# First block's attention by tile, and stick-breaking attention in twelve batches of 512 columns, in an eight-stage transformer kernel

## The chip, the cores and the metric
The kernel runs on one core of a Trainium2 chip, all in fp32. A core has TensorE (PE, matmuls), VectorE (DVE), ScalarE (ACT, activation functions), GpSimd (POOL, which here issues the gathers) and SyncE (SP, which issues the loads), 16 DMA engines, an SBUF of 128 partitions and a PSUM of eight banks of 512 fp32 columns. The engines run their own instruction streams and wait for one another on semaphores. The metric is the device time in microseconds, lower is better.

## The reference
Two transformer blocks over 256 tokens of width 1024, one batch. The change lies in the first block, which has two layers:

```python
def first_block(x, ...):
    for layer in range(2):
        if layer < 1:
            mix = _diff_attention(x, ...)          # 8 heads with two maps each, softmax, sublayer norm
        else:
            k_sb, v_sb = _shared_kv(x, w_kv_b)
            mix = _stick_breaking(x, ...)          # 16 heads of 64
        x = _layer_norm(DEEPNORM_ALPHA * x + mix, ...)
        x = _layer_norm(DEEPNORM_ALPHA * x + _peer(x, ...), ...)

# stick-breaking, for a block of 128 queries
    mask = key_pos[None, :] < t[:, None]
    z = einsum('bhqd,bhkd->bhqk', q, k_sb) * scale
    log_one_minus = where(mask, log_sigmoid(-z), 0.0)
    tail = cumsum(log_one_minus, reverse=True) - log_one_minus
    a = where(mask, exp(log_sigmoid(z) + tail), 0.0)
    out = einsum('bhqk,bhkd->bhqd', a, v_sb)
```

`_diff_attention` takes per head the difference of two softmax maps (keys of later 64-token chunks are masked), multiplies by v, divides each head's 128 outputs by their root mean square (the sublayer norm) and projects. `_peer` scores 8 heads of 2 x 128 sub-keys per token, picks 16 experts of each head by two top-16 selections, fetches a row of 2048 numbers (u and v) for each of the 128 picks, takes gelu(x.u) times a gate, and adds up the v's. The second block has four layers (selected, window, latent and again selected attention), each with an MLP of width 4096.

## The kernel before
**Layout.** T = 256 tokens are two tiles (NT = 2) of P = 128. `x` holds the tokens by partition, `xT` the same turned, `y` is 3 x 1024 columns per tile for projections. `weights` has four slots of 2 MB; a slot takes a chunk of 512 columns of a weight matrix. `arena` (8192 columns) holds attention outputs `o` or four gathered rows, `heads_arena` holds `qT` and `kT`, `scratch` small work.

**Semaphores and order.** Each engine's order is written out by hand. A planner at the top gives every PSUM use a `Group` (bank, number of its filling, number of its freeing) and every weight chunk the event after which its slot is free (`slot_release`). PE waits `bank_free(g)` before it fills and `copied(g)` where it needs the evicted data; the others wait `filled(g)`. SP issues the weight loads in program order (`load_weights`, L780).

**Building blocks.** `turns` (L870) transposes four 128x128 blocks through a bank, ACT evicts them (L1233). `project` (L883) makes one block of 512 output columns for one tile: 8 matmuls over the 1024 inputs, 16 in the trace, as each fp32 matmul shows as two. ACT evicts it to `y` (L1239) or DVE adds it to x (`add_to_x`, L1688). `project_turned` (L893) makes PEER queries already turned. `layer_norm` (L1695 to L1701) is DVE with a square root on ACT (`root`, L1243). A change of function on ACT costs a table load.

**First stage.** qkv projection of both tiles; rotation; turns; `attend(diff)` runs 32 units (16 maps x 2 tiles) as a software pipeline: scores of unit i (L916), transposes of probabilities of unit i-2 (L931), values of unit i-4 (L942), with DVE negating, masking and taking the maximum (L1654), copying (L1667) and dividing each four units (L1677, L1679), ACT exponentiating (L1251). Then DVE does the sublayer norm of tile 0 and 1 (L2068 to L2075), PE turns both, projects tile 0 and 1 (4 blocks), and `peer` begins.

**PEER stage.** Per tile: turn x, project queries, scores against the sub-keys (L1000), evictions (L1301). Then DVE routes (`route`, L1711 to L1752), POOL gathers (L2173; ten slots of 1 MB, four in `arena`, six in weight slots 1 to 3), DVE takes the products (L1770), ACT gelu (L1311) and diagonal matrices of the weights (L1320), PE mixes the v's (L1018). `PE_PICKS` says which picks PE mixes: all 16 of each head. `peer_sum` in `xT` starts as ALPHA times x (L1807); at a tile's end `add_mixed` (L1793) adds the banks to it, and a layer norm follows. Weight slots 1 to 3 are released by that norm.

**Stick attention.** PE waits for both tiles of x, turns them, projects keys and values (8 blocks) and queries (4 blocks), turns queries and keys, then `stick_attend` runs 16 heads of 384 columns (keys 0 to 127 x 256 queries, keys 128 to 255 x 128 queries):

```python
    z^T = k q^T                                   # PE, L954, L955, 64 rows deep
    l = log(1 + exp(-|z|))                        # ACT, L1266, L1268, L1278
    w = max(z, 0) + l; sp = w * mask; w = z - w   # DVE, L1842, L1843, L1845
    t = later^T sp (+ ones^T sp of later tile)    # PE, L965 to L968
    w = w - t                                     # DVE, L1851
    a = exp(w) * mask                             # ACT L1285, POOL L2196
    o += a^T v                                    # PE, L979 to L981
```

The heads' exponentials and logarithms go in fours, since each change of function reloads a table. Then turns of `o`, output projection (4 blocks), two norms, and the second PEER stage.

## Time and profile before
| | us |
|---|---|
| median of 3 runs | 3105.93 (3105.5 to 3109.35) |
| the profiled execution, its own time | 3107.64 |
| its span, first to last instruction | 3106.0 |
| PE / PEld / DVE / ACT / POOL busy | 2616.1 / 1611.5 / 1741.4 / 917.0 / 648.9 |
| mean DMA rate over the span | 247 GB/s |
| granted TensorE clock, mean | 0.953 |

The span begins with the first instruction. PE is the matmul unit, PEld its weight loads, which overlap it. A share of busy time is a mean over stages of different kinds: two PEER stages with gathers, four MLPs, and attention. The page's second part cuts the span into 40 slices of 78 us. A timeline row reads: start, duration, engine, line, operation, output<-inputs, shapes, count, and in brackets the idle time before it with what ended it.

### The profile page before, as it was taken

How to read it: one execution, taken by the hardware profiler on the slowest of the kernel's cores; microseconds unless marked ns; L12 is line 12 of the kernel's file. 1: busy time of each engine (PE TensorE's matmuls, PEld its weight loads, DVE VectorE, ACT ScalarE, POOL GpSimd, SP SyncE). 2: the span in 40 equal slices, each digit the busy share in tenths (PEclk: the TensorE clock that was granted, in tenths of full speed). 3: DMA queues.
4: the chain of work that ended last, by engine and by line, in shares of the span. 5: the costliest groups of instructions: out<-in, count | busy, mean ns of one | idle time of the engine just before them, and what ended most of it. 6: DMA issues, size and time to landing. Idle time of an engine off the chain costs nothing.

```text
span 3106.0 us, 30124 instructions
## 1 busy us (share of the span) xinstructions
PE 2616.1 (84%) x10349; PEld 1611.5 (52%) x10349; DVE 1741.4 (56%) x3866; ACT 917.0 (30%) x1914; POOL 648.9 (21%) x635
## 2 busy tenths in 40 slices
PE   7986777777779796777777788999999989998999
PEld 3553222223334662222222234798479857985698
DVE  2446777777630446777777645654455455545554
ACT  1312222222112421222222123443344354433443
POOL 0004444444410203444444411000100000001000
PEclk9998999999989698999999999999999989999999
DMA  7219999999964019999999953354335423543253
GB/s 249 82 30 399 422 421 416 389 421 421 421 268 157 1 62 414 421 421 421 386 421 421 421 204 109 121 185 154 109 124 188 151 82 122 189 159 109 96 189 108
DMA packets 209663, 767.63 MB, mean 247 GB/s; under 512 B 16435, under 2 KB 87686, under 8 KB 143750
## 3 DMA queue, kind: packets, MB, share of 16 engines
q0 software_dynamic: 73760, 536.93, 41.7%
q1 hardware_dynamic: 135782, 229.22, 22.0%
q8 instruction: 60, 0.98, 0.1%
q14 instruction: 61, 0.50, 0.0%
HBM read 765.03 MB, written 1.07 MB: 247 GB/s over the span
## 4 chain that ended last, share of the span: by engine, by line
PE 39%; DMA 6%; DVE 4%; ACT 1%; issue 1%; POOL 0%; DVEq 0%; ACTq 0%
PE psum L1056 12%; PE psum L1070 11%; PE psum L883 9%; DMA weights<-in_peer_uv,scratch 4%; DMA arena<-in_peer_uv,scratch 2%; PE psum L1018 2%; PE psum L942 1%; PE psum L870 1%; PE psum L931 1%; PE psum L920 1%; DVE heads_arena L1770 1%; PE psum L916 0%; PE psum L1034 0%; DVE arena L1679 0%; ACT scratch L1320 0%
## 5 line engine op out<-in xcount | busy, mean ns | idle before, releaser
L1018 PE MATMUL psum<-weights,scratch 128*128 128x512 f32 x1224 | 585.5, 624 | 203.6 <-ACT scratch L1320 203.6
L883 PE MATMUL psum<-weights,xT 128*128 128x512 f32 (+2 forms) x1192 | 517.8, 593 | 16.4 <-ACT xT L1233 11.4
L1018 PEld LDWEIGHTS psum<-weights,scratch 128*128 128x128 f32 x1224 | 229.4, 196 | 558.4 <-ACT scratch L1320 306.9
L1018 PE MATMUL psum<-arena,scratch 128*128 128x512 f32 x824 | 391.0, 620 | 133.6 <-ACT scratch L1320 132.9
L2173 POOL DMA_INDIRECT weights<-in_peer_uv,scratch x306 | 342.2, 1118 | 498.9 <-PE psum L1018 407.5
L1995 DVE TENSOR_TENSOR piece<-weights,piece 128x2048 fp32r<-128x2048 f32 x128 | 292.8, 2293 | 221.1 <-ACT piece L1361 221.1
L1056 PE MATMUL psum<-split_x,piece 128*128 128x256 f32 x3072 | 385.4, 286 | 6.2 <-DVE split_x L2002 6.2
L1056 PEld LDWEIGHTS psum<-split_x,piece 128*128 128x128 f32 x3072 | 383.4, 195 | 11.6 <-issue 7.6
L883 PEld LDWEIGHTS psum<-weights,xT 128*128 128x128 f32 x1192 | 228.7, 196 | 284.1 <-issue 273.5
L1070 PE MATMUL psum<-piece,hidden 128*128 128x512 f32 x1536 | 358.8, 390 | 0.0
L1311 ACT ACTIVATE scratch<-scratch 128x2 f32<-128x2 f32 x256 | 52.1, 203 | 1000.2 <-DVE heads_arena L1770 1000.2
L1018 PEld LDWEIGHTS psum<-arena,scratch 128*128 128x128 f32 x824 | 153.2, 195 | 370.0 <-ACT scratch L1320 201.6
L2173 POOL DMA_INDIRECT arena<-in_peer_uv,scratch x206 | 230.9, 1121 | 413.1 <-PE psum L1018 285.3
L1070 PEld LDWEIGHTS psum<-piece,hidden 128*128 128x128 f32 x1536 | 284.8, 188 | 56.8
L1361 ACT ACTIVATE piece<-weights 128x2048 fp32r<-128x2048 f32 x128 | 243.2, 1906 | 170.1 <-PE psum L1056 170.1
L1770 DVE SCALAR_TENSOR_TENSOR heads_arena<-weights,x 128x1024 f32<-128x1024 f32 x153 | 187.3, 1224 | 131.0 <-DMA weights<-in_peer_uv,scratch 131.0
L1770 DVE SCALAR_TENSOR_TENSOR scratch<-weights,x 128x1024 f32<-128x1024 f32 x153 | 187.4, 1225 | 89.4 <-issue 81.5
L1770 DVE SCALAR_TENSOR_TENSOR heads_arena<-arena,x 128x1024 f32<-128x1024 f32 x103 | 126.1, 1224 | 84.5 <-DMA arena<-in_peer_uv,scratch 84.4
L1320 ACT ACTIVATE scratch<-const,scratch 128x128 f32<-128x128 f32 x512 | 173.3, 386 | 0.0
L2209 POOL MEMSET heads_arena<- 64x256 f32 (+1 forms) x6 | 3.1, 521 | 776.5 <-DVE arena L1875 776.3
L1770 DVE SCALAR_TENSOR_TENSOR scratch<-arena,x 128x1024 f32<-128x1024 f32 x103 | 126.1, 1225 | 59.6 <-issue 51.2
L1239 ACT ACTIVATE y<-psum 128x512 f32<-128x512 f32 (+1 forms) x52 | 29.9, 576 | 249.3 <-PE psum L883 249.3
(206 smaller groups left out, 2346.8 us busy)
## 6 DMA issues: line engine op xcount, KB each, us to landing
weights<-in_w_up SPq DMA_DIRECT2D x64, 1024.0 KB, 5.5
weights<-in_w_down SPq DMA_DIRECT2D x64, 1024.0 KB, 4.9
weights<-in_w_qkv_a SPq DMA_DIRECT2D x6, 2048.0 KB, 20.2
weights<-in_a_w_in SPq DMA_DIRECT2D x6, 2048.0 KB, 10.4
weights<-in_peer_w_q SPq DMA_DIRECT2D x4, 2048.0 KB, 8.4
weights<-in_w_kv_b SPq DMA_DIRECT2D x4, 2048.0 KB, 12.9
weights<-in_a_w_out SPq DMA_DIRECT2D x4, 2048.0 KB, 8.6
weights<-in_b_w_in SPq DMA_DIRECT2D x3, 2048.0 KB, 10.3
```

The costliest lines, as they stand in the source:

```text
L870: mm = pe.transpose(psum[g.bank][0:rows, j * P:j * P + n], src, identity[0:n, 0:n])
L883: mm = pe.matmul(psum[g.bank][:, 0:w], xT[:, block0 + k, t * P:(t + 1) * P], c.view[:, k, c0:c0 + w], start=(k == 0), stop=(k == c.rows - 1))
L920: pe.matmul(psum[g.bank][:, 0:2 * nk], qT[:, h // 2, t * P:(t + 1) * P], paired_keys(kind, h, nk), start=True, stop=True).then_inc(psum_fi ...
L1018: mm = pe.matmul(psum[g.bank][:, :], diagonal[:, j % DIAGONALS, :], row[:, D + half * BANK:D + (half + 1) * BANK], start=(j == pe_picks(t ...
L1056: mm = pe.matmul(psum[g.bank][:, b * T:(b + 1) * T], w[a][:, k, b * P:(b + 1) * P], split_x[c][:, k, :], start=(k == 0 and (a, c) == PARTS ...
L1070: mm = pe.matmul(psum[g.bank][:, :], h[a][:, k, t * P:(t + 1) * P], w[c][:, k, half * BANK:(half + 1) * BANK], start=(first and k == 0 and ...
L1311: act.activation(gelu[:, k:k + 2], dots[:, k:k + 2], ACT.Gelu).then_inc(gelu_given.sem, 1)
L1320: act.activation(diagonal[:, j % DIAGONALS, :], identity, ACT.Copy, scale=weight[:, k:k + 1])\
L1361: act.activation(split_piece[n][0][:, :], raw_piece[n], ACT.Copy).then_inc(high_ready.sem, 1)
L1770: dve.scalar_tensor_tensor(unused[at % 2], gathered[at % GATHER_SLOTS][:, 0:D], 1.0, x[:, n // SEL, :], ALU.mult, ALU.mult, accum_out=dots ...
L1995: dve.tensor_tensor(split_piece[n][1][:, :], raw_piece[n], split_piece[n][0][:, :], ALU.subtract)\
L2173: pool.indirect_dma_start(gathered[at % GATHER_SLOTS], None, rows, bass.IndirectOffsetOnAxis(ap=expert[:, t, k:k + 1], axis=0), element_of ...
```

## The change
1. **Diff attention by tile.** `attend` on PE and DVE is called once per tile. Tile 0's sublayer norm is a generator whose six pieces DVE does inside tile 1's units (`SUBLN_STEPS`), in `y` instead of `heads_arena`; ACT takes its root after eight of tile 1's exponentials. Turns and output projection go by tile, with the turn of x tile 0 for PEER between the last two blocks.
2. **PEER entry.** `queries` and `scores_of` replace the first half of `peer`: the turn of x tile 1 comes before the scores of tile 0. The branch for picks not mixed by PE leaves, with `peer_sum`; `add_mixed` does x = ALPHA * x + bank. Weight slots 1 to 3 are released by the last mixing.
3. **Stick attention.** Twelve batches of 512 columns: for tile 0 four heads of one key tile, for tile 1 two heads of two key tiles. Keys and queries are projected turned for both tiles at once (`project_both`), ACT writes them to `kT` and to `stick_q`, where each pair of heads has its other half zeroed by POOL, so scores are 128 rows deep. The mask is a matmul of -1e30 with an identity, in fp32r, into the same bank. Values go to PSUM turned (`stick_oT`), so no turn precedes the output projection. The second halves of values, keys and queries and tile 0's output projection stand between rounds of three batches.
4. **Constants** are 256 columns narrower.

The diff, cut to its core:

```diff
+STICK_BATCHES = ((0, 0), (0, 4), (1, 0), (1, 2), (1, 4), (1, 6), (0, 8), (0, 12), (1, 8), (1, 10), (1, 12), (1, 14))
+SUBLN_STEPS, SUBLN_ROOT = (2, 4, 6, 9, 11, 13), 8
...
-                slot_release[1] = slot_release[2] = slot_release[3] = (x_ready.sem, ln_x[2 * layer + 1] + NT)
+                slot_release[1] = slot_release[2] = slot_release[3] = (value_mixed.sem, self.mixed0 + NT * SEL)
...
+                self.s = [group(2 + b % 3) for b in range(n)]
+                self.t = [group(5) for _ in range(n)]
...
+            def project_both(c, g, half):
+                bank_free(g)
+                for j in range(2):
+                    at = (2 * half + j) * P
+                    for k in range(KB):
+                        mm = pe.matmul(psum[g.bank][:, j * T:(j + 1) * T], c.view[:, k, at:at + P], xT[:, k, :],
+                                       start=(k == 0), stop=(k == KB - 1))
...
+            def stick_scores(s, b):
+                t, h = STICK_BATCHES[b]
...
+                if t == 0:
+                    pe.matmul(psum[g.bank][:, :], stick_identity[:, :], stick_masks[:, :], start=True, stop=False)
+                for j in range(2):
+                    pair, keys = (h // 2 + j, 0) if t == 0 else (h // 2, j)
...
+                    mm = pe.matmul(psum[g.bank][:, j * T:(j + 1) * T], kT[:, pair, keys * P:(keys + 1) * P], stick_q[t][:, pair, :, :],
...
+            def stick_later(s, b):
...
+                if t == 0:
+                    mm = pe.matmul(psum[g.bank][:, :], later, w, start=True, stop=True)
+                else:
+                    pe.matmul(psum[g.bank][:, T:2 * T], later, w[:, T:2 * T], start=True, stop=True)
+                    pe.matmul(psum[g.bank][:, 0:T], later, w[:, 0:T], start=True, stop=False)
+                    mm = pe.matmul(psum[g.bank][:, 0:T], ones, w[:, T:2 * T], start=False, stop=True)
...
-            attend(diff, "diff")
-            pe.wait_ge(in_ready.sem, diff_out_in + 1)
-            turns(diff_out_turn)
-            copied(diff_out_turn.last)
-            project(diff_out.blocks)
-            peer(peer0, ln_x[0])
+            attend(diff, "diff", 0, HEADS)
+            attend(diff, "diff", HEADS, NT * HEADS)
+            for t in range(NT):
+                pe.wait_ge(in_ready.sem, diff_out_in + t + 1)
+                turns(diff_out.turn[t])
+                project(diff_out.blocks[t][0:1], turned=diff_out.turn[t].done)
+                if t == NT - 1:
+                    turn_x(peer0, 0, ln_x[0])
+                project(diff_out.blocks[t][1:2])
+            queries(peer0, ln_x[0])
...
+            exps(diff, None, 0, HEADS + SUBLN_ROOT)
+            root(diff_root, PEER_HEADS)
+            exps(diff, None, HEADS + SUBLN_ROOT, NT * HEADS)
+            root(diff_root + 1, PEER_HEADS)
+            for t in range(NT):
+                turns(diff_out.turn[t])
...
+                for first in range(0, len(STICK_BATCHES), 3):
+                    batches = range(first, first + 3)
+                    softs(batches)
+                    logits(batches)
+                    less_later(batches)
```

PE's order in the stick attention is now: x turn 0, values 0 (tile 0), x turn 1, values 0 (tile 1), keys 0, queries 0, scores of batches 0 to 2, values 1 (2 blocks), later sums 0 to 2, half of keys 1, scores 3 to 5, values of 0 to 2, half of keys 1 and of queries 1, later sums 3 to 5, rest of queries 1, scores 6 to 8, values 3 to 5, later sums 6 to 8, scores 9 to 11, values 6 to 8, output block, later sums 9 to 11, output block, values 9 to 11; then the two output blocks of tile 1 with the turn of x tile 0 between. ACT's order has the same rounds: logs, Ln, evictions, Exp.

**PE, from the end of the diff attention to the first mixing.** L870/L904 are turns (by what they read: `arena` the attention's output, `x`, `heads_arena` the sub-keys), L883/L917 the output projection, L893/L927 queries, L1000/L1110 scores. Before:

```order
L942 MATMUL psum<-y,scratch 128x128 x6
L870 MATMUL psum<-const,arena 128x128 x16
L883 MATMUL psum<-weights,xT 128x512 x32
L870 MATMUL psum<-const,x 128x128 x8
L870 MATMUL psum<-const,heads_arena 128x128 x8
L893 MATMUL psum<-xT,weights 128x128 x64
L1000 MATMUL psum<-heads_arena 128x128 x16
L870 MATMUL psum<-const,x 128x128 x8
L893 MATMUL psum<-xT,weights 128x128 x64
```

And now:

```order
L976 MATMUL psum<-y,scratch 128x128 x6
L904 MATMUL psum<-const,arena 128x128 x8
L917 MATMUL psum<-weights,xT 128x512 x16
L904 MATMUL psum<-const,arena 128x128 x8
L917 MATMUL psum<-weights,xT 128x512 x8
L904 MATMUL psum<-const,x 128x128 x8
L917 MATMUL psum<-weights,xT 128x512 x8
L904 MATMUL psum<-const,heads_arena 128x128 x8
L927 MATMUL psum<-xT,weights 128x128 x64
L904 MATMUL psum<-const,x 128x128 x8
L1110 MATMUL psum<-heads_arena 128x128 x16
L927 MATMUL psum<-xT,weights 128x128 x64
```

The turns stand by tile, and both turns of x moved ahead by one step.

**PE, where the third round of stick batches begins.** L1002 and L1006 are masks, L1007 scores, L1037 values, L1019 to L1023 sums over later keys, L986 turned projections, L917 plain ones. Before, the same place had single heads in a pipeline, nine instructions to a head:

```order
L954 MATMUL psum<-heads_arena 128x256
L955 MATMUL psum<-heads_arena 128x128
L965 MATMUL psum<-arena,const 128x128
L966 MATMUL psum<-arena,const 128x128
L967 MATMUL psum<-arena,const 128x128
L968 MATMUL psum<-arena,const 128x128
L979 MATMUL psum<-y,arena 128x64
L980 MATMUL psum<-y,arena 128x64
L981 MATMUL psum<-y,arena 128x64
```

And now:

```order
L986 MATMUL psum<-xT,weights 128x256 x16
L1002 MATMUL psum<-stick_masks,stick_identity 128x512
L1007 MATMUL psum<-y,heads_arena 128x256 x2
L1002 MATMUL psum<-stick_masks,stick_identity 128x512
L1007 MATMUL psum<-y,heads_arena 128x256 x3
L1006 MATMUL psum<-stick_masks,stick_identity 128x256
L1007 MATMUL psum<-y,heads_arena 128x256
L1037 MATMUL psum<-arena,y 64x128 x12
L1019 MATMUL psum<-arena,const 128x512 x2
L1021 MATMUL psum<-arena,const 128x256
L1022 MATMUL psum<-arena,const 128x256
L1023 MATMUL psum<-arena,const 128x256
```

Between scores (L1007) and later sums (L1019) of this round stand only the value matmuls of the round before.

**DVE, inside tile 1's units of the diff attention.** L1654/L1823 is the masked maximum, L1667/L1836 the copy of transposed probabilities. Before, two units:

```order
L1654 ISA scratch,neg_max<-psum,const 128x256
L1654 ISA neg_max 128x1
L1667 COPY scratch<-psum 128x256
L1654 ISA scratch,neg_max<-psum,const 128x256
L1654 ISA neg_max 128x1
L1667 COPY scratch<-psum 128x256
```

And now:

```order
L2219 SCALAR_TENSOR_TENSOR y<-arena,lam 128x1024
L1823 ISA scratch,neg_max<-psum,const 128x256
L1823 ISA neg_max 128x1
L1836 COPY scratch<-psum 128x256
L1823 ISA scratch,neg_max<-psum,const 128x256
L1823 ISA neg_max 128x1
L1836 COPY scratch<-psum 128x256
L2221 TENSOR_TENSOR y<-y 128x1024
```

A piece of tile 0's norm over 1024 columns stands before every second or third unit.

## Rows read from the trace of the kernel before

**Rows 1.** Page, part 2: granted clock of TensorE and share of the DMA engines
```profile
PEclk9998999999989698999999999999999989999999
...
DMA  7219999999964019999999953354335423543253
```

**Rows 2.** Windows: busy PE, PEld, DVE, ACT, POOL, clock, DMA share, GB/s
```profile
262.00:551.00 289.00, 219.61 (x468) 86.04 (x466) 208.88 (x550) 65.01 (x199) 134.30 (x118) 0.98 1.00 415
...
260.00:264.00 4.00, 4.00 (x7) 1.61 (x6) 3.93 (x11) 1.30 (x6) 1.63 (x1) 0.66 0.40 152
...
923.00:996.00 73.00, 72.31 (x171) 31.90 (x170) 0.00 (x0) 6.57 (x11) 0.00 (x0) 1.00 0.45 161
1019.00:1024.00 5.00, 0.00 (x0) 0.00 (x0) 1.97 (x4) 4.49 (x9) 1.95 (x2) 0.65 0.00 0
1024.00:1085.00 61.00, 51.04 (x221) 46.01 (x222) 25.54 (x48) 23.65 (x41) 15.20 (x14) 0.55 0.00 1
```

**Rows 3.** Timeline, DVE: two units of the attention's second tile
```profile
137.56 0.42 DVE L1654 CUSTOM_DVE_ANT_0 scratch<-psum,const 128x256 f32<-128x256 f32 x1 [0.65 <-PE psum L916]
...
137.93 0.42 DVE L1667 COPY scratch<-psum 128x256 f32<-128x256 f32 x1
...
139.00 0.42 DVE L1654 CUSTOM_DVE_ANT_0 scratch<-psum,const 128x256 f32<-128x256 f32 x1 [0.65 <-PE psum L916]
```

**Rows 4.** Timeline, DVE: sublayer norm, first tile's sum and norm
```profile
153.55 1.28 DVE L2068 SCALAR_TENSOR_TENSOR heads_arena<-arena,lam 128x1024 f32<-128x1024 f32 x1
...
157.38 0.17 DVE L2071 TENSOR_SCALAR root_in<-sums 128x8 f32<-128x8 f32 x1
...
185.82 0.69 DVE L1688 SCALAR_TENSOR_TENSOR x<-x,psum 128x512 f32<-128x512 f32 x1 [6.25 <-PE psum L883]
...
190.97 1.23 DVE L1701 TENSOR_TENSOR x<-x,ln_gb 128x1024 f32<-128x1024 f32 x1
```

**Rows 5.** Timeline, PE: turns, output projection, first queries
```profile
167.64 3.39 PE L870 MATMUL psum<-const,arena 128*128 128x128 f32 x16 [15.06 <-DVE arena L2075]
171.71 27.73 PE L883 MATMUL psum<-weights,xT 128*128 128x512 f32 x64 [0.69 <-ACT xT L1233]
...
201.56 14.46 PE L893 MATMUL psum<-xT,weights 128*128 128x128 f32 x128
```

**Rows 6.** Timeline, POOL: first and eleventh gather; first of the second PEER stage
```profile
230.02 1.00 POOL L2173 DMA_INDIRECT arena<-in_peer_uv,scratch  x1 [119.82 <-DVE scratch L1752]
...
261.49 1.63 POOL L2173 DMA_INDIRECT arena<-in_peer_uv,scratch  x1 [16.98 <-PE psum L1018]
...
1151.72 0.97 POOL L2173 DMA_INDIRECT weights<-in_peer_uv,scratch  x1 [67.13 <-DVE scratch L1752]
```

**Rows 7.** Timeline, PE: last mixing, turns, twelve projection blocks, scores after a stall
```profile
894.79 3.60 PE L1018 MATMUL psum<-weights,scratch 128*128 128x512 f32 x8
905.57 3.68 PE L870 MATMUL psum<-const,x 128*128 128x128 f32 x16 [7.18 <-DVE x L1701]
909.93 85.02 PE L883 MATMUL psum<-weights,xT 128*128 128x512 f32 x192 [0.69 <-ACT xT L1233]
...
1024.17 1.22 PE L954 MATMUL psum<-heads_arena 64*128 64x256 f32 x2 [5.43 <-DVE scratch L1845]
```

**Rows 8.** Timeline, PE: output projection of the stick attention
```profile
1091.29 29.86 PE L883 MATMUL psum<-weights,xT 128*128 128x512 f32 x64 [0.69 <-ACT xT L1233]
```

**Rows 9.** Timeline, ACT: eviction of the second key and value block
```profile
926.32 0.60 ACT L1239 ACTIVATE y<-psum 128x512 f32<-128x512 f32 x1 [6.27 <-PE psum L883]
```

**Rows 10.** Groups by form, 885 to 1152 us: prices
```profile
L954 PE MATMUL psum<-heads_arena 64*128 64x256 f32 x32 | 13.9, 566 | 11.9 <-DVE scratch L1845 10.7 <-ACT heads_arena L1233 1.1
...
L1268 ACT ACTIVATE arena<-arena 128x384 f32<-128x384 f32 x16 | 8.4, 523 | 0.4
...
L1268 ACT ACT_TABLE_LOAD x4 | 5.1, 1283 | 0.1
...
L1688 DVE SCALAR_TENSOR_TENSOR x<-x,psum 128x512 f32<-128x512 f32 x4 | 2.7, 687 | 26.6 <-PE psum L883 26.6
```

More of the change, by code:

```diff
@@ new lines, in stick_outputs, with stick_values @@
+            def stick_outputs(s, g):
+                t, half = g % NT, g // NT
+                last = max(b for b in range(len(STICK_BATCHES)) if s.out_of(b) == g)
+                act.wait_ge(unit_done.sem, s.done0 + last + 1)
+                to = s.out[g]
+                act.activation(stick_oT[:, 4 * half:4 * half + 4, t * P:(t + 1) * P],
+                               psum[to.bank][:, :].rearrange("p (b t) -> p b t", t=P), ACT.Copy).then_inc(psum_freed[to.bank], 1)
+            def stick_values(s, blocks):
+                outputs(blocks, lambda t, at, w: y[:, t, 2 * D + at:2 * D + at + w])
@@ L1638, in attend @@
                 for i in range(first, last + 5):
[L1639 to L1640 removed]
+                    if between:
+                        between(i - first)
                     if i < last:
```

587 lines of the change are left out of this document (328 added, 259 removed).

## The prediction
> **What bounds the kernel now.** I read the page's slices first [rows 1]. In slices 5 to 11 and 16 to 23 the DMA engines are full (9 of 10). These are the gathers of the two PEER stages, and inside them no engine sets the pace: from 262 to 551 us the DMA share is 1.00 while PE is busy 219.6 of 289 us and DVE 208.9 [rows 2]. 256 gathers of 1 MB at 415 GB/s are about 645 us, twice. The change alters none of them, so a PEER stage counts by where its first gather stands. Three stretches are left in which it can act: up to the first gather, from the last mixing of the first stage to the first gather of the second, and the joints. The MLPs behind keep their order and only move along.
>
> In the first stretch PE is full in the attention: a unit of the second tile takes 1.44 us (137.56 to 139.00), of which DVE is busy some 0.92 [rows 3]. Then DVE alone does the sublayer norm of both tiles, 7.0 us each: it starts at 153.55 [rows 4] and PE turns from 167.64. 27.7 us of output projection follow, the queries start at 201.56 [rows 5], the first gather at 230.02 [rows 6]. In the second stretch PE ends the mixing at 898.4, waits for x until 905.6, projects keys, values and queries from 909.9 to 995.0 and does the stick attention until 1086 [rows 7]. There it stalls 5.4 us, and its clock falls from 2.4 to 1.2 GHz: granted 1.00 from 923 to 996, 0.55 from 1024 to 1085, where PE is busy 51 of 61 us [rows 2]. The output projection runs from 1091.3 to 1121.2 [rows 8], the first gather starts at 1151.7 [rows 6].
>
> **First stretch.** Output projection, norm and turns now go by tile.
> - The attention is split: PE and DVE finish tile 0 before tile 1's first scores. The overlap of four units is lost. Bounds: nothing, and four units of 1.44 us, 5.8. I take 3, since a first-tile unit is shorter and some work fills the gap.
> - Tile 0's norm, 6.5 us without its gaps, goes between tile 1's units. DVE has 0.52 us to spare in each of twelve units and spends 0.7 to 0.9 on output after every fourth: about 3.7 free. 2.8 stay, less what the three-deep buffers absorb. On ACT the square root costs two table loads of 1.28 us. Together 2 (0 to 5.6). The attention's last output is then at 158.5 instead of 153.5.
> - PE turns tile 0 at once, but ACT evicts only after tile 1's root, which DVE asks for 4.0 us into its norm [rows 4]: 162.7. The projection starts at 163.9 instead of 171.7. After 13.9 us, tile 1's turn (2.0, half of the 4.1 in rows 5), a block of 6.9, the turn of x (1.0) and the last block, it ends at 194.7 instead of 199.4: 4.7 gained. The norm of tile 0 (from 185.8 to 192.2 before [rows 4]) is ready before its turn.
> - From there to the first gather it took 30.6 us, now 0.8 less: of the 2.1 between projection and queries one turn leaves, while tile 1's turn enters before the scores and covers the wait for the query's eviction.
> - The eleventh gather came at 261.5, 31.5 us after the first, and the DMA share sank to 0.40 for 4 us [rows 2, 6]. Tile 1's queries no longer wait for a turn (1.8 us earlier), so of the 2.4 idle us 2 go. The constants are 128 KB shorter: 0.3 at 415 GB/s.
>
> Sum: 4.7 + 0.8 + 2 + 0.3 = 7.8, with bounds of 1 and 13.
>
> **Second stretch.** I follow PE, for everything it does stands in one order, and add each wait. A block of 8 x 512 columns costs 6.87 us (0.60 + 6.27 between evictions, [rows 9]); the turned blocks have the same columns. From 898.4:
> - DVE frees the banks, turn of x 0: 2.8; value block 6.9; turn of x 1: 2.0 (x is ready at 908: ACT loads the root's table late, but PE is busy); value block 6.9. That is 916.9, where before the second block ended at 926.3. Slots 1 to 3 are released 7 us earlier and their loads are hidden.
> - First key and query halves, 4 blocks: 27.5, 944.4. Before, all twelve blocks stood here and 5 us of turns behind them; the turns are gone.
> - Wait for four ACT copies: 1.8. Scores of three batches: 512 columns each at 0.43 us per 256 (the pair of passes; the mean of 566 ns [rows 10] overlaps and is half in slow clock), masks 0.12 to 0.25: 3.2. Second values, 2 blocks: 13.7, which covers ACT and DVE.
> - Sums over later keys, first round: 3.0 of PE, but all twelve go through bank 5, so each waits for DVE's subtraction of its forerunner, 0.69 [rows 10] and some 0.3 of signals: 5.0. Keys 6.9, scores 3.0, values 2.6, two blocks 13.7, later sums 3 x 1.28 + 2.0 = 5.8, block 6.9, ACT copies 1.8, scores 3.2, values 2.6: 1014.6.
> - Third round: nothing covers. ACT loads Ln's table, 1.28, and does 3 x 0.6 (384 columns took 0.52); DVE does six operations of 0.69 before the first subtraction. PE waits 3.2, then about 3.3 after its first sum and 0.8 after the second; with 3.0 of work: 1024.9.
> - Scores 3.0, values 2.6, output block 6.9, later sums 5.8, block 6.9, values 2.6, block 6.9, turn of x 1.0, block 6.9: 1067.5, instead of 1121.2. At full clock 53.7 gained, and 0.8 to the gather as above.
> - Clock. A pause of 5.4 us took it away [rows 2, 7]. In the third round two pauses of over 3 us stand close together, with one short sum between, so I expect it to fall there. After 1091 the projection cost 29.9 instead of 27.5 [rows 8]: continuous work brings it back at a price of 2.4. Until the output block some 12 us run at half clock: 5 lost. Bounds 0 and 22 (every burst up to the last block, 15, and 2.4 at each of three blocks).
> - DMA: the third gather waited for the queries of tile 1, earlier now by 1.5: 1.3 gained. POOL's masking leaves; its four memsets come behind the last gather, 50 us ahead of their use.
>
> Sum: 53.7 + 0.8 - 5 + 1.3 = 50.8, with bounds of 34 and 56.
>
> The Trainium skill (ScalarE: Activation LUTs, What ACT_TABLE_LOAD costs) adds to each switch of tables a drain of about 1.38 us. The rows speak against it: 1283 ns for the load, and 0.4 us of idle time ahead of all sixteen exponentials behind four such loads [rows 10]. By the page the exposed switches, two or three, would make the time 3 to 4 us longer.
>
> In all 7.8 + 50.8 = 58.6 us. The profiled execution took 3107.6, which gives 3049; it is 1.7 above the median of the runs shown, so on that scale **3047**. Layer 0 of the second block finds three slots released 7 us earlier, where it did not wait: nothing.
>
> **Rivals.**
> 1. The clock stays down from the third round: not 5 but 22 us are lost, 3064. For it: 61 us at 0.55 with PE busy 84% of them [rows 2]. Against: four whole blocks now stand between the bursts. 0.12. The Trainium skill (TensorE: Matmul & The Clock Gate, HAM oscillation) describes just this, bursts with waits between them that are slowed each time; the trace agrees for the old attention, and no run here shows it with projections between.
> 2. The first stretch gives nothing: split 3, interleaving 9.3 unabsorbed, the attention ends at 165.8, the projection at 201.7, 2.3 later than before. With the other terms of the stretch, 3.1, about 1 us remains: 3054. For it: units on PE are back to back, so each lateness shows. Against: DVE idles a third of them. 0.14.
> 3. Slower than before: the projections do not cover the rounds, because PE waits in its order ahead of each. A round by itself is scores 3, ACT 5, Ln 3, DVE 4, sums 6, Exp 3, values 3: 27, four of them 108; with 16 blocks, 110, and 9 of turns and waits 227, and with 20 for the old clock 247, against the 223 from 898.4 to 1121.2. Less the 9.9 gained elsewhere, 14 are lost: 3120. It decides once the four rounds wait some 59 us more than reckoned. Against: between scores and sums stand two blocks in round 1 and two in round 2. 0.02.
> 4. Better: no fall of the clock, and the attention absorbs the norm: 3037 to 3042. 0.08.
>
> **Numbers.** The forecast holds 0.64. The range takes in its bounds, rivals 2 and 4: 3033 to 3064; left out are half of rival 1 and all of rival 3. A difference of 0.2% (6.2 us) is about what can be told from none: faster 0.97, the same 0.01, slower 0.02.
>
> **What would show it.** First gather at 222 (220 to 229). PE at 160 to 164 idle, then projecting by tile. Value block right behind the mixing at about 901. Key and query halves until 944, waits of 1 us between later sums, a gap near 1014 to 1023 on the shifted clock and a granted clock below 1 there only; the output projection ends 174 us (at most 185) behind the mixing's end instead of 223; first gather 29.8 later. Wrong would be: waits of over 5 us ahead of a projection in rounds 1 or 2, a clock of 0.5 through rounds 3 and 4, or gathers that do not keep 415 GB/s.

## The result, and the profile after

| | before | after |
|---|---|---|
| median, us | 3105.72 (3102.51 to 3109.35, 4 executions) | 3059.15 (3054.74 to 3059.78, 4 executions) |
| after / before | | 0.9847, 95% interval 0.983 to 0.9864 |
| profiled execution, its time / its span | 3107.64 / 3106.0 | 3059.78 / 3058.1 |
| first gather of the first PEER stage | 230.02 | 236.25 |
| end of that stage's mixing, behind it | 668.4 | 668.4 |
| first gather of the second stage, behind the mixing's end | 253.3 | 198.4 |
| from that second gather to the end of the span | 1954.3 | 1955.1 |
| granted TensorE clock, mean | 0.953 | 0.961 |

The change is faster by 46.6 us. The forecast was 3047, 58.6 faster, and its range of 3033 to 3064 holds the result. The table shows where the 12 us lie: the second stretch gave 55.0 (forecast 49.5 to this point), while the first gather, forecast by the sum at 5.5 earlier (4.7 + 0.8), came 6.2 later, and the 2.3 that the sum put behind it did not come.

Page of the changed kernel, part 2, the rows that answer to [rows 1]:

```profile
PEclk9888999999999999999999999999999989998999
DMA  7208999999984169999999931553355324543353
```

The dip of the clock in the stick attention (the 6 of before, in slice 14) is gone. A new, shallower one stands in slices 2 and 3 (88 in place of 99).

Windows of the changed kernel, columns as in [rows 2] (busy PE, PEld, DVE, ACT, POOL, clock, DMA share, GB/s):

```profile
130.00:134.00 4.00, 2.95 (x15) 1.72 (x15) 3.36 (x10) 1.15 (x5) 0.00 (x0) 1.00 0.00 0
134.00:140.00 6.00, 6.00 (x20) 3.90 (x20) 5.03 (x14) 2.35 (x8) 0.00 (x0) 0.55 0.01 3
140.00:150.00 10.00, 10.00 (x32) 6.82 (x32) 4.36 (x15) 5.18 (x11) 0.00 (x0) 0.50 0.00 1
...
165.00:168.00 3.00, 3.00 (x16) 3.00 (x15) 1.62 (x4) 0.90 (x1) 0.00 (x0) 0.50 0.00 0
...
169.00:170.00 1.00, 0.94 (x9) 0.70 (x7) 0.86 (x2) 0.00 (x0) 0.00 (x0) 1.00 0.00 0
...
1022.00:1026.00 4.00, 2.08 (x2) 0.50 (x2) 4.00 (x7) 2.16 (x3) 0.00 (x0) 0.51 0.00 0
```

PE is idle for 1 of 4 us at the joint between the attention's two tiles. From then on it is busy all the time, at half the clock, until some 168.6, in the attention's last matmuls. Timeline of PE there, the joint and then one unit (scores, transposes, values):

```profile
130.01 0.49 PE L976 MATMUL psum<-y,scratch 128*128 128x128 f32 x2 [0.42 <-DVE scratch L1836]
130.43 1.13 PE L950 MATMUL psum<-heads_arena 64*128 64x256 f32 x6
132.59 0.44 PE L965 MATMUL psum<-const,scratch 128*128 128x128 f32 x2 [1.04 <-ACT scratch L1355]
...
146.56 1.22 PE L950 MATMUL psum<-heads_arena 64*128 64x256 f32 x2
147.71 0.69 PE L965 MATMUL psum<-const,scratch 128*128 128x128 f32 x2
148.19 1.06 PE L976 MATMUL psum<-y,scratch 128*128 128x128 f32 x4
149.18 1.22 PE L950 MATMUL psum<-heads_arena 64*128 64x256 f32 x2
```

Two pauses, 0.42 and 1.04 us, and a unit then takes 2.62 us (146.56 to 149.18) in place of 1.44 [rows 3]. DVE writes the attention's last output at 169.32 to 170.01 and begins the norm at 170.04; before, the norm behind the attention began at 153.55 [rows 4]. A kernel does not reach its attention at the same time in each profile, so stretches are better counted from the attention's first scores. PE began them here at 114.15, and before at 113.61:

```profile
113.61 0.71 PE L916 MATMUL psum<-heads_arena 64*128 64x128 f32 x6 [1.06 <-ACT heads_arena L1233]
```

So the attention took 39.9 us to the norm before, and 55.9 now.

Timeline, PE: output projection and the first stick block; POOL: the gathers that answer to [rows 6]:

```profile
174.92 16.00 PE L917 MATMUL psum<-weights,xT 128*128 128x512 f32 x32 [4.98 <-ACT xT L1337]
...
906.87 7.11 PE L917 MATMUL psum<-weights,xT 128*128 128x512 f32 x16 [0.18 <-ACT xT L1337]
```

```profile
236.25 1.00 POOL L2333 DMA_INDIRECT arena<-in_peer_uv,scratch  x1 [125.50 <-DVE scratch L1921]
...
267.59 1.38 POOL L2333 DMA_INDIRECT arena<-in_peer_uv,scratch  x1 [17.40 <-PE psum L1123]
...
1103.02 0.95 POOL L2333 DMA_INDIRECT weights<-in_peer_uv,scratch  x1 [216.13 <-DVE scratch L1921]
...
1107.49 0.94 POOL L2333 DMA_INDIRECT weights<-in_peer_uv,scratch  x1 [2.29 <-PE psum L927]
```

Timeline, PE: the third round of stick batches, and the end of the output projection:

```profile
1017.68 1.58 PE L1037 MATMUL psum<-arena,y 128*64 128x128 f32 x24
1022.62 2.08 PE L1019 MATMUL psum<-arena,const 128*128 128x512 f32 x2 [3.35 <-DVE arena L1995]
1026.29 2.05 PE L1019 MATMUL psum<-arena,const 128*128 128x512 f32 x2 [1.60 <-DVE arena L2010]
1029.28 1.19 PE L1021 MATMUL psum<-arena,const 128*128 128x256 f32 x2 [0.94 <-DVE arena L2010]
...
1066.23 7.03 PE L917 MATMUL psum<-weights,arena 128*128 128x512 f32 x16
```

The last block ends at 1073.1, 168.5 behind the mixing's end at 904.66; it was 222.8 before and forecast at 174. The waits of the third round are 3.35, 1.60 and 0.94, against 3.2, 3.3 and 0.8 in the forecast. Of the 1.7 by which the second is shorter, 1.1 went into the first sum itself, 2.08 at half clock in place of 1.02 (the same sum in the first round, at 968.62).

### The profile page after: what moved, and what is told of

The parts are those of the page before. It is cut to its first block, busy times and chain, and to the rows that moved or that the text cites. A ratio compares the mean times of both kernels' runs of the same rounds, so it can differ in the third digit from the quotient of the medians.

```text
span 3058.1 us, 29977 instructions
## 1 busy us (share of the span) xinstructions
PE 2584.2 (85%) x10337; PEld 1604.8 (52%) x10337; DVE 1706.0 (56%) x3830; ACT 917.5 (30%) x1906; POOL 623.6 (20%) x623
## 3 DMA queue, kind: packets, MB, share of 16 engines
q0 software_dynamic: 73760, 536.93, 42.4%
## 4 chain that ended last, share of the span: by engine, by line
PE 40%; DMA 6%; DVE 3%; ACT 1%; issue 1%; POOL 0%; DVEq 0%; ACTq 0%; POOLq 0%
PE psum L1161 12%; PE psum L1175 11%; PE psum L917 9%; DMA weights<-in_peer_uv,scratch 4%; PE psum L1123 2%; DMA arena<-in_peer_uv,scratch 2%; PE psum L976 1%; PE psum L904 1%; PE psum L965 1%; PE psum L954 1%; PE psum L950 0%; DVE heads_arena L1939 0%; PE psum L1139 0%; DVE arena L1848 0%; DVE xT L2030 0%
## 5 line engine op out<-in xcount | busy, mean ns | idle before, releaser
L1123 PE MATMUL psum<-weights,scratch 128*128 128x512 f32 x1224 | 576.3, 616 | 202.8 <-ACT scratch L1494 202.8
L2333 POOL DMA_INDIRECT weights<-in_peer_uv,scratch x306 | 335.4, 1096 | 643.3 <-PE psum L1123 406.8
L917 PE MATMUL psum<-weights,xT 128*128 128x512 f32 (+2 forms) x1000 | 437.8, 596 | 19.7 <-ACT xT L1337 14.7
L917 PEld LDWEIGHTS psum<-weights,xT 128*128 128x128 f32 x1000 | 193.6, 198 | 240.6 <-issue 233.0
L1355 ACT ACTIVATE scratch<-scratch,neg_max 128x128 f32<-128x128 f32 (+1 forms) x160 | 72.4, 453 | 91.7 <-DVE neg_max L1823 88.9
```

What stands on the lines that cost most here:

```text
L917: mm = pe.matmul(psum[g.bank][:, 0:w], source[:, block0 + k, t * P:(t + 1) * P], c.view[:, k, c0:c0 + w], start=(k == 0), stop=(k == c.row ...
L1123: mm = pe.matmul(psum[g.bank][:, :], diagonal[:, n % DIAGONALS, :], row[:, D + half * BANK:D + (half + 1) * BANK], start=(k == 0), stop=(k ...
L1355: act.activation(probs[:, u % 3, 0:nk], neg_logits[:, u % 3, 0:nk], ACT.Exp, bias=neg_max[:, u:u + 1], scale=-1.0, accum_out=row_sum[:, u: ...
L2333: pool.indirect_dma_start(gathered[at % GATHER_SLOTS], None, rows, bass.IndirectOffsetOnAxis(ap=expert[:, t, k:k + 1], axis=0), element_of ...
```

## The experiments

Two things were open: why the first stretch lost, and why the eleventh gather still came 31.3 us behind the first (31.5 before, 29.5 forecast). All runs were timed beside before, whose medians were 3106.22, 3108.16 and 3106.65 in the three groups of runs. One mark has to be known for what follows: the kernels bridge, hold, round3 and banks are the same up to the first gather, which came at 221.45, 223.51, 222.62 and 220.86. A difference of under 3 us between two single profiles says nothing there. Nearly all of this spread lies ahead of the attention: from its first scores to the first gather these four took 110.4, 110.5, 110.2 and 110.1. Counted so, before took 116.4 and the change 122.1. The way from the first gather to the mixing's end was 665.2 to 669.0 in the ten profiles without held gathers.

### joined

```diff
-            attend(diff, "diff", 0, HEADS)
-            attend(diff, "diff", HEADS, NT * HEADS)
+            attend(diff, "diff")
```

PE, DVE and ACT alike, with both norms and both roots behind.

> The change, but with the diff attention undivided on PE, DVE and ACT as before, and both sublayer norms behind it; turns and output projection stay by tile. Joint theory (in the changed kernel PE drained between tile 0 and tile 1, idle for 0.4 and 1.0 us, the granted clock fell from 1.00 to 0.50 there and stayed until the attention's end): the clock holds, a unit of tile 1 takes 1.44 us again, the attention's last output comes at 153.5; then norm 7, root of tile 1 asked 4 us into the second norm, so the output projection starts near 167, the first gather near 227, total 3050 (9 less than the change). Weaving theory (the clock fell because DVE's pieces of norm made PE wait): the same 227 and 3050, as the weaving is gone as well; split_plain tells them apart. Chance theory (the clock can fall in any attention of this kind, and happened to): a clock of 0.5 in one of them anyway, first gather above 236, total 3060 or more.

Measured: 3046.59 (3041.96 to 3049.72), ratio 0.981 [0.9793, 0.9826]. The clock is 1.00 to the attention's end, the first gather came at 226.00, 113.3 behind the first scores. So the projection by tile alone is worth 3.1 of the first stretch, as expected (227 for the gather), and the two edits that were to bring more, split and weaving, took 8.8 away.

### split_plain

```diff
-            attend(diff, "diff", None, None, HEADS, NT * HEADS, lambda i: next(first_norm, None) if i in SUBLN_STEPS else None)
+            attend(diff, "diff", None, None, HEADS, NT * HEADS)
+            for _ in sublayer_norm(0):
+                pass
```

> The change, split into two attentions, but with tile 0's norm not woven in: both norms stand behind, and both roots. Joint theory: the clock falls at the joint just the same, units of 2.62 us, the attention's last output near 169 as in the change, and 7 us of norm are no longer hidden: projection starts near 182, first gather near 243, total 3066. Weaving theory: the clock holds, the split costs 3 us, last output near 156.5, first gather near 230, total 3053.

Measured: 3062.59 (3049.8 to 3064.18), ratio 0.9849 [0.9824, 0.9874]; first gather 242.81. Windows of its profiled execution:

```profile
130.00:134.00 4.00, 2.96 (x9) 1.42 (x8) 2.61 (x11) 2.19 (x8) 0.00 (x0) 0.73 0.02 4
134.00:140.00 6.00, 6.00 (x19) 3.67 (x18) 1.79 (x7) 1.21 (x4) 0.00 (x0) 0.50 0.00 0
```

The clock falls at the same place with nothing woven in. It fell at some 131.9 here and at some 134.6 in the change, each time within about 2 us of the pause of 1.04 us. The weaving theory falls and the joint theory stands: 243 was expected for the gather, and the total is 3.4 under the 3066. One of the four executions took 3049.8 with a mean clock of 0.966 (the others 0.959 to 0.963): that is near the time expected where the clock holds (3053), so it seems that these pauses take the clock in most executions and not in all. No trace of that execution was kept, so this is not shown.

### bridge

```diff
+                    if kind == "diff" and i in (HEADS, HEADS + 2) and first == HEADS:
+                        keep_clock(att.v[HEADS // att.per], 1 if i == HEADS else 2)
```

`keep_clock(g, n)` issues n matmuls of 128x512 on constants into a bank whose contents are not used yet. It is no invention of this run: the kernel of before has, among others, two such matmuls ahead of tile 0's first transposes and eight in the old stick attention; the change kept the first two and dropped the eight.

> The change, with three matmuls of 128x512 on constants added at the joint (one before tile 1's first scores, two before its first transposes), split and weaving as in the change. Joint theory: PE does not pause, the clock holds at 1.00, a unit takes 1.44 to 1.6 us, the attention's last output is at 158 to 160 instead of 170, first gather near 224, total 3047. Weaving theory: the clock still falls once DVE's pieces of 1.2 us stand between the units; first gather 236, total 3059. If PE loses its clock for another reason at that place (the small matmuls themselves), likewise 3059 or more.

Measured: 3045.95 (3043.26 to 3046.89), ratio 0.9806 [0.9789, 0.9822]. Windows; the first gather; the attention's first scores and a later pause; the start of the last norm:

```profile
130.00:134.00 4.00, 4.00 (x16) 2.00 (x17) 3.72 (x10) 1.81 (x6) 0.00 (x0) 1.00 0.00 0
134.00:140.00 6.00, 6.00 (x37) 4.20 (x35) 5.46 (x18) 3.08 (x9) 0.00 (x0) 1.00 0.02 4
```

```profile
221.45 1.00 POOL L2335 DMA_INDIRECT arena<-in_peer_uv,scratch  x1 [113.79 <-DVE scratch L1923]
```

```profile
111.06 0.71 PE L950 MATMUL psum<-heads_arena 64*128 64x128 f32 x6 [1.06 <-ACT heads_arena L1339]
...
142.80 0.44 PE L967 MATMUL psum<-const,scratch 128*128 128x128 f32 x2 [0.50 <-ACT scratch L1357]
```

```profile
154.58 1.29 DVE L2221 SCALAR_TENSOR_TENSOR y<-arena,lam 128x1024 f32<-128x1024 f32 x1
```

Three matmuls that compute nothing make the kernel 13.2 us faster. With them the first gather comes 110.4 us behind the first scores, 6.0 sooner than before; the sum had 5.5. The last norm begins 43.5 behind the first scores, before it was 39.9: split and weaving together cost 3.6 of the 5 that I had reckoned (3 and 2). The total is only level with that of joined (3046.59), which has neither split nor weaving.

Only the pause of 1.04 us was filled. The 0.42 at the joint is still there, and one of 0.50 at 142.80, where ACT takes the root; the granted clock was 1.00 through both, here and in the six later kernels that have this bridge. The 1.06 ahead of the first scores, with `keep_clock`'s two matmuls soon behind it, did not take the clock in any profile either.

### woven and woven_bridge

```diff
-SUBLN_STEPS, SUBLN_ROOT = (2, 4, 6, 9, 11, 13), 8
+SUBLN_STEPS, SUBLN_ROOT = (21, 23, 25, 28, 30, 32), 9
...
-            attend(diff, "diff", None, None, HEADS, NT * HEADS, lambda i: next(first_norm, None) if i in SUBLN_STEPS else None)
+            attend(diff, "diff", None, None, 0, NT * HEADS, lambda i: next(first_norm, None) if i in SUBLN_STEPS else None)
```

> The change, with the attention undivided, tile 0's norm woven between the units 21 to 32 of the 32 (tile 0's last output is written at step 20), its root after 25 exponentials. Joint theory: clock 1.00 throughout, last output near 155.5 (2 us for the weaving), root of tile 1 asked 4 us later, projection starts near 161, first gather near 221, total 3044, the best of the four. Weaving theory: DVE's pieces make PE wait, the clock falls after step 21, and the attention ends near 165 or later: first gather 231, total 3054.

Measured: 3045.16 (3044.9 to 3062.89), ratio 0.9823 [0.9792, 0.9855]; first gather 225.59. Timeline, PE: it paused for ACT's root, and 2 us later a unit was slow:

```profile
143.70 0.44 PE L965 MATMUL psum<-const,scratch 128*128 128x128 f32 x2 [1.44 <-ACT scratch L1354]
...
146.36 1.22 PE L950 MATMUL psum<-heads_arena 64*128 64x256 f32 x2
```

There is no joint here, yet the clock fell at some 145.7, behind one pause of 1.44 us. The joint theory was too narrow: a pause elsewhere in this attention can do it too. The fall came some 12 us later than in the change (counted from the first scores) and the clock was back at some 155, so it cost less. For woven_bridge the pause was filled:

```diff
+                    if kind == "diff" and i == 27:
+                        keep_clock(att.v[6], 2)
```

> The kernel woven (undivided attention, tile 0's norm between its later units), with two matmuls of 128x512 on constants ahead of the transposes of unit 25, where PE had waited 1.44 us for ACT's square root with its two table loads and where the granted clock fell from 1.00 to 0.50 some 2 us later. Pause theory (any wait of about 1 us in the attention, at the joint or at the root, takes the clock): the clock holds until the attention's end, last output near 153 to 156, first gather near 219 instead of 225.6, total 3041 to 3043, and no execution above 3050 (woven had one at 3062.9). If DVE's pieces of 1.2 us take it: the clock falls at the same place, first gather 225 or later, total 3045.

Measured: 3043.88 (3043.1 to 3045.63), ratio 0.9794 [0.9778, 0.981]. The clock was 1.00 in every window from 116 to 155, and no execution stood out. The last norm begins 42.4 behind the first scores (woven 45.7, joined 39.9), so weaving, with the two matmuls, costs 2.5 at full clock, where 2 was forecast. The first gather came at 222.25, not at 219: the projection still began at 159.92, behind the same wait for ACT, which the next run takes away.

### turn_first

```diff
+            turns(diff_out.turn[0])
             root(diff_root + 1, PEER_HEADS)
-            for t in range(NT):
-                turns(diff_out.turn[t])
+            turns(diff_out.turn[1])
```

on top of bridge.

> The kernel bridge, with ACT evicting tile 0's turn before it takes tile 1's root. In bridge PE waited 4.98 us for that eviction (the output projection began at 159.45) and then ran its first block at half clock. If ACT's order is the wait: the projection starts near 156, 3.4 earlier, and with a pause of 2 us in place of 5 perhaps at full clock (another 2 to 3 us); first gather 216 to 218 instead of 221.45, total 3040 to 3043. Rival: tile 0's projection now stands beside tile 1's norm, but tile 1's turn and the adding to x come no earlier, since DVE works on the norm until 161.6: then less than 2 us, total 3044 to 3046.

Measured: 3039.14 (3035.69 to 3039.83), ratio 0.9778 [0.9762, 0.9794]; first gather 216.26. Timeline, PE, of bridge and of turn_first:

```profile
159.45 16.66 PE L917 MATMUL psum<-weights,xT 128*128 128x512 f32 x32 [4.98 <-ACT xT L1339]
```

```profile
156.96 13.97 PE L917 MATMUL psum<-weights,xT 128*128 128x512 f32 x32 [0.34 <-ACT xT L1339]
```

Counted from the first scores (111.06 and 113.11) the projection starts 4.5 earlier, and it ends another 2.7 earlier by the clock: two blocks cost 16.66 behind a pause of 5 us and 13.97 behind one of 0.34. The first gather comes 7.2 earlier by the same count, and the median fell by 6.8.

### hold

```diff
+                        if p.layer == 0 and n == 2:
+                            pool.wait_ge(psum_filled[p.q.groups[1][1].bank], p.q.groups[1][1].filled)
```

on top of bridge. In the traces of before, the change and bridge ACT's last eviction of tile 1's queries came 11.6, 11.5 and 11.5 us behind the first gather, wherever PE stood.

> The kernel bridge, with POOL holding the third gather of the first PEER stage until PE has projected tile 1's queries, as it happens by itself in the second stage. In bridge ACT's last eviction of these queries and the ninth gather both went on only 11.5 us after the first gather, though PE had ended its projection 4.6 us after it, and the DMA share fell to 0.32 for 4 us before the eleventh gather (31.4 us after the first; in the second stage 22.9). Theory: eight gathers queued at once delay something that passes through the same DMA engines and frees ACT. Then ACT evicts at once, the eleventh gather comes 23 to 27 us after the first, the gap of 3.7 us goes and 1 to 2 us of late gathers are paid: total 3042 to 3044, mixing end 2 to 3 us closer to the first gather (661.9 in bridge). Rival: the delay is tied to the program and not to the gathers: ACT still waits until 11.5 us after the first gather, and the held gathers cost 2: total 3048.

(The 661.9 in it is counted to the start of the last unbroken run of mixing matmuls; to their end bridge took 669.0, and the other kernels 665.2 or more.)

Measured: 3039.53 (3038.69 to 3040.77), ratio 0.9779 [0.9763, 0.9795]. Timeline, ACT, of bridge, and the window ahead of its eleventh gather:

```profile
232.99 0.60 ACT L1460 ACTIVATE heads_arena<-psum 128x512 f32<-128x512 f32 x1 [13.37 <-remote]
```

```profile
252.00:256.00 4.00, 4.00 (x9) 1.65 (x8) 3.97 (x16) 1.58 (x6) 2.25 (x2) 0.80 0.32 66
```

And of hold, the same two with the third and the eleventh gather:

```profile
228.24 0.60 ACT L1460 ACTIVATE heads_arena<-psum 128x512 f32<-128x512 f32 x1 [6.55 <-PE psum L927]
```

```profile
228.47 0.94 POOL L2337 DMA_INDIRECT arena<-in_peer_uv,scratch  x1 [2.72 <-PE psum L927]
...
246.17 1.20 POOL L2337 DMA_INDIRECT arena<-in_peer_uv,scratch  x1 [7.15 <-PE psum L1125]
```

```profile
244.00:248.00 4.00, 4.00 (x9) 1.74 (x8) 2.04 (x6) 0.79 (x3) 1.32 (x2) 0.80 1.02 424
```

ACT evicts as soon as PE is done, the eleventh gather stands 22.7 us behind the first in place of 31.4, the DMA share stays at 1.0, and the mixing ends 662.3 behind the first gather. Issuing the third and later gathers of the first ten later (2.4 us for the third to the eighth) made the kernel 6.4 us faster. The four kernels with this hold took 661.5 to 662.3 for the stage; bridge, with 669.0, was the longest of the ten without it, so the stage's own gain lies between 2.9 and 7.
### round3

```diff
+                keep_clock(s.out[2], 4)
                 for b in (6, 7, 8):
                     stick_later(s, b)
+                    if b < 8:
+                        keep_clock(s.out[2], 1)
```

on top of bridge.

> The kernel bridge, with four matmuls of 128x512 on constants ahead of the third round's first sum over later keys (PE had waited 3.35 us there) and one after each of the first two sums (waits of 1.60 and 0.94). In the change the granted clock fell to 0.50 from 1022 to 1030 and the three sums took 9.3 us from the first to the scores. Theory: no pause, no fall, the sums take 6 to 7 us; from the mixing's end to the second stage's first gather 195.5 instead of 198.4, total 3042 to 3044. Rival: the round is bound by ACT and DVE and not by PE's clock: 198.4 stays, or grows by 1 where the added matmuls stand in the way, total 3046.

Measured: 3042.66 (3041.16 to 3044.36), ratio 0.979 [0.9774, 0.9807]. From the mixing's end to the second stage's first gather it took 195.9 in place of 198.4, and the clock stayed at 1.00. The fall in the third round had cost 2.5.

### banks

```diff
-                self.t = [group(5) for _ in range(n)]
+                later = (5, 0, 1)
+                self.t = [group(bank) for bank in later]
...
+                self.t += [group(5), group(0), group(1)]
...
+                self.t += [group(bank) for bank in later]
+                self.t += [group(5) for _ in range(3)]
```

on top of bridge, with the groups of the second key and query halves planned between, in PE's order.

> The kernel bridge, with the sums over later keys of the first three rounds going to banks 5, 0 and 1 in turn, in place of all to bank 5 (the fourth round stays in bank 5). In bridge each sum after the first of a round waited 0.94 us for DVE's subtraction of its forerunner (1.60 once). If that is PE's loss: two waits less in each of three rounds, 1.9 us in rounds 1 and 2 each and 2 to 3 in round 3, less what the evictions behind then wait: from the mixing's end to the second stage's first gather 193 to 195 instead of 198.4, total 3040 to 3042. Rival: DVE and ACT set the pace of the round, and what PE gains at the sums it waits at the values or at the next scores: 197 to 198, total 3045.

Measured: 3035.17 (3033.13 to 3035.99), ratio 0.9771 [0.9755, 0.9787]. Timeline, PE, the first round's sums, of bridge and then of banks:

```profile
954.46 1.02 PE L1021 MATMUL psum<-arena,const 128*128 128x512 f32 x2
956.42 1.10 PE L1021 MATMUL psum<-arena,const 128*128 128x512 f32 x2 [0.94 <-DVE arena L2012]
958.46 0.67 PE L1023 MATMUL psum<-arena,const 128*128 128x256 f32 x2 [0.94 <-DVE arena L2012]
```

```profile
950.69 1.88 PE L1030 MATMUL psum<-arena,const 128*128 128x512 f32 x4
952.41 0.59 PE L1032 MATMUL psum<-arena,const 128*128 128x256 f32 x2
```

The way from the mixing's end to the second first gather is 191.8, 6.6 less than in bridge. In the first round DVE and ACT kept up, and the one bank had held PE; in the second round one wait of 0.43 (for ACT) and one of 0.94 remain, and the fourth round was left as it was. The median gained 10.8 over bridge, more than these 6.6; 3.2 of it is in the first PEER stage, inside its spread.

### four, all_bridge and all_woven

bridge with turn_first, hold and round3; that with banks; and the last on the attention of woven_bridge.

> The kernel bridge with turn_first, hold and round3 together. Each acts in its own stretch, so the gains over bridge (3045.95) should add: 6.8 by the order of ACT's eviction, 6.4 by the held gathers, 3.3 by the third round: 3029.5, first gather near 216.5, eleventh 22.7 behind it, 195.8 from the mixing's end to the second stage's first gather. If they do not add (an earlier first gather meets the hold at another point, or the DMA engines set the stage's end whatever its start): 3033 or more.

> The kernel four, with the three banks of the kernel banks besides. If the waits on bank 5 are PE's loss beside the held clock too: 3 to 4 us under the kernel four, 3026; if DVE sets the round: the same as four. Next to it, banks alone tells which.

> The same as all_bridge, but with the attention undivided and tile 0's norm woven between its later units, with the bridge at the root's wait (woven_bridge) in place of the bridge at the joint. Woven_bridge ended its attention at 154.6 where bridge ended at 155.0 or so, so the two should come out within 1 us of one another: 3026. If the undivided pipeline is worth its four overlapping units once nothing else waits: 2 to 3 us under all_bridge.

| | us | ratio to before |
|---|---|---|
| four | 3028.81 (3028.15 to 3029.95) | 0.9749 [0.9733, 0.9765] |
| all_bridge | 3021.17 (3021.02 to 3023.26) | 0.9727 [0.9711, 0.9743] |
| all_woven | 3023.41 (3021.1 to 3025.5) | 0.9731 [0.9715, 0.9747] |

The gains add (3029.5 expected). Banks beside them gave 7.6, not 3 to 4: with it the way from the mixing's end to the second first gather is 190.8 in place of 195.9. The rest lies in places that the edit does not touch, 1.6 up to the first gather, 0.6 in the first PEER stage and 1.4 behind the second first gather, and is not shown to be its work. Undivided or split makes no difference that can be told once neither pauses. **all_bridge** is the best version found: 38.0 us under the change, 85.5 under the before of its runs.

## Why the prediction was right or wrong

The total was held by the range, but as a sum of one stretch that was better and one that failed, and that is luck: the range reached down to 3064 for a clock lost elsewhere, half of rival 1. The two sums' own lower bounds, 1 and 34, add up to 3071, which the range did not take in although the text says so.

- **First gather, 5.5 earlier; it was 6.2 later.** The step that failed is "The attention's last output is then at 158.5". It priced the split by the work that no longer overlaps (3, with 5.8 as the end) and the weaving by DVE's time (2). These prices were of the right size: bridge shows 3.6 for both, woven_bridge 2.5 for the weaving. What was missing is that the joint made PE pause for 0.42 and 1.04 us, and with this the clock was down for 34 us of short matmuls; the last output was at 170.0 in place of 158.5. I had read the clock's rows for the old stick attention only [rows 2] and put the price of a pause into the third round and not here, although the attention of before runs PE without a gap, with a unit at 1.44 us [rows 3] that took 2.62 at half clock. The end of the range for this term, 5.8, should have been a second tile at half clock: twelve and more units at 2.62 less 1.44. Measured, the change's attention took 12.4 more than bridge's (55.9 and 43.5).
- **From the attention's end to the first gather.** In bridge, where the clock held, the attention began 2.5 sooner than in before, by no edit; with these 2.5 added, the projection starts at 162.0 (forecast 163.9) behind the forecast order of waits (turn, root, eviction), ends at 194.6 (194.7), and the gather comes 29.4 later (29.8), at 224.0. That fits the sum, which gives 224.5. The sign "first gather at 222" counted the 2.3 in that the sum puts behind the gather, so bridge's 221.45 met it by chance. What I left out is that the first two blocks behind a pause of 5 us run in part at half clock, 2.7.
- **Eleventh gather, 2.** Nothing came of it. The step laid the gap of DMA share to PE's late queries. PE was early and ACT's eviction was not; hold shows that the gathers issued by then made the gap. The rows to see it stood in the trace of before: the eviction came 11.6 us behind the first gather, while PE's block had ended 5 us before that.
- **Second stretch, 49.5 to the first gather; 55.0.** It was 5.5 better than forecast. The walk along PE held nearly step by step: key and query halves ended at 45.3 behind the mixing's end (forecast 46.0), waits of 0.94 between sums, the pause ahead of the third round of 3.35 (3.2). Better than forecast were the values of three batches, 1.5 and not 2.6 (four times), and the clock's fall, 2.5 and not 5: it was back at some 1032, before the output block. The 0.9 for a sum's wait was right too, and was a loss that could be removed.
- **Third gather, 1.3.** Its idle time went from 4.58 to 2.29, but the way from the second first gather to the end grew by 0.8; nothing of it can be told in the total. Timeline, POOL, of before:

```profile
1158.52 0.94 POOL L2173 DMA_INDIRECT weights<-in_peer_uv,scratch  x1 [4.58 <-PE psum L893]
```

- **ACT's tables.** No drain: the load began right behind the activation ahead of it, took 1.28, and the next activation began 1.30 behind its start. Timeline, ACT, of the change:

```profile
953.01 0.60 ACT L1371 ACTIVATE arena<-psum 128x512 f32<-128x512 f32 x1 [1.45 <-PE psum L1007]
953.62 1.28 ACT L1373 ACT_TABLE_LOAD   x1
954.92 0.63 ACT L1373 ACTIVATE arena<-arena 128x512 f32<-128x512 f32 x1
```

  The 3 to 4 us that the figure of the Trainium skill (ScalarE: Activation LUTs, What ACT_TABLE_LOAD costs) would have added to the time are not there.
- **Rivals.** Rival 1 had the right mechanism, a clock lost in pauses between bursts and not regained, at the wrong place: in the stick attention the clock was back by 1034, and in the diff attention only at its very end (168.6). Rival 2 had the right place, the attention's end (165.8, measured 170.0), by a cause that was not it. Rival 3 did not come near deciding. Rival 4, no fall at all and the norm absorbed, did not come: even in woven_bridge, with the clock held, the norm costs 2.5. Bridge comes to 3046 and not to 3042, since the clock still falls ahead of the projection and in the third round.

## What to carry to other kernels

Where PE works on small matmuls back to back, a new gap of about 1 us in its order can cost far more than itself: here 12.4 us behind gaps of 0.42 and 1.04, 3.3 behind one of 1.44, and nothing behind single gaps of 0.42 to 0.56. The length alone does not tell which it will be, so look at the granted clock behind each new gap, price its end of the range by the whole run of small matmuls behind it at half clock, and try a few matmuls on constants in the gap before giving the order up. Count stretches from a mark that the edit does not move: two profiles of the same work stood 2.2 us apart before the attention began. When a wait in the trace stays at nearly the same distance from a burst of DMAs, whatever the engine it is put down to does, suspect the burst, and try issuing less of it at once. A PSUM bank that takes all results of a kind in turn makes its producer wait for its consumer each time; look for the same short wait repeated.

## What the hardware did that was not expected

- Once fallen, the clock stayed down in the change's diff attention although PE was busy in every microsecond from 134 to 168 us (granted 0.50 from 140 on). It was back at some 168.6, while PE did the attention's last values, with no scores between them; woven (some 155) and split_plain (some 166) show the same place. In the wait of 5 us ahead of the output projection it fell again, and was back from 179 us on.
- The same pause did not take the clock in each execution: one of four of split_plain seems to have held it, one of four of woven (3062.89, mean clock 0.959 against 0.964 to 0.966) seems to have lost it earlier than the others. With the long pauses filled, none of the last nine kernels spread by more than 4.4 us.
- With eight gathers of 1 MB issued 1.25 us apart, an eviction on ACT went on only 10.1 to 11.6 us behind the first, and the ninth gather 10.3 to 11.9, both with "remote" as the releaser. What the eviction waits for by the program, the end of PE's second query block, lay 5 to 7 us back.
